# Earlier transposes behind the output projection, and gated MLP weights a chunk ahead, in a two-layer DiT block

## The reference, cut to what matters

```python
x = _layer_norm(DEEPNORM_ALPHA * x + g_a * y, ln1_g[l], ln1_b[l])
x = _layer_norm(DEEPNORM_ALPHA * x + g_m * _squared_relu_mlp(x * (1 + sc_m) + sh_m, mlp_w1[l], mlp_w2[l]),
                ln2_g[l], ln2_b[l])
```

## Time and profile before

| | us |
|---|---|
| median of 3 runs | 3045.91 (3042.36 to 3052.49) |
| profiled execution | 3046.93 |
| its span | 3045.1 |
| around the span | 1.8 |
| PE busy in the span | 2802.1 |
| DVE, ACT, POOL busy | 1397.4, 878.6, 559.6 |
| layer 0 projection begins (first large loads issued) | 524.8 |
| layer 1 projection begins | 2184.3 |
| layer 1, first matmul of the MLP / first second product | 2297.6 / 2337.5 |

### The profile page before, as it was taken

The page is one execution under the profiler, slowest core; times in us unless marked ns, Lnnn a source line. Parts: engine busy times, 40 slices in busy tenths (PEclk is TensorE's granted clock), DMA queues, the critical chain, the costliest instruction groups (busy, mean ns, idle before and its releaser), DMA issues. The chain is left out here.

```text
span 3045.1 us, 40518 instructions
## 1 busy us (share of the span) xinstructions
PE 2802.1 (92%) x15572; PEld 2288.9 (75%) x15572; DVE 1397.4 (46%) x2153; ACT 878.6 (29%) x1684; POOL 559.6 (18%) x375
## 2 busy tenths in 40 slices
PE   5999993999999999999957999999698999999997
PEld 2666783778888888888845888888576888888886
DVE  3575435563333333333383555555555433333345
ACT  4243323342111121121224344343433211121222
POOL 0000002232112121121140000000033323233231
PEclk6999996999999999999977999999999999999999
DMA  6575214541101011010033111110356111111112
GB/s 219 195 301 166 73 52 158 165 132 49 35 28 55 28 41 41 28 55 28 30 122 96 42 36 49 36 36 8 105 131 173 48 46 44 55 41 41 55 41 56
DMA packets 192607, 238.90 MB, mean 78 GB/s; under 512 B 15960, under 2 KB 153776, under 8 KB 186352
## 3 DMA queue, kind: packets, MB, share of 16 engines
q1 hardware_dynamic: 192208, 237.29, 24.4%
q10 hardware_dynamic: 288, 0.10, 0.0%
HBM read 203.70 MB, written 37.88 MB: 79 GB/s over the span
## 5 line engine op out<-in xcount | busy, mean ns | idle before, releaser
L2054 DVE TENSOR_TENSOR y<-y,pair 128x1024 f32<-128x1024 f32 x280 | 340.1, 1219 | 314.1 <-PE pair L2161 314.1
L2159 PE MATMUL pair<-m_wbh,m_ath 128*128 128x512 f32 x1152 | 452.6, 393 | 15.0 <-DVE y L2054 8.4
L2161 PE MATMUL pair<-m_wbh,m_atl 128*128 128x512 f32 x1152 | 451.2, 392 | 0.0
L2160 PE MATMUL pair<-m_wbl,m_ath 128*128 128x512 f32 x1152 | 450.0, 391 | 0.0
L2103 DVE TENSOR_TENSOR m_atl<-m_sq,m_ath 128x512 fp32r<-128x512 f32 x160 | 138.4, 866 | 664.9 <-POOL m_sq L1972 664.0
L1932 ACT ACTIVATE m_rel<-pair 128x512 f32<-128x512 f32 x160 | 88.9, 556 | 996.7 <-PE pair L2183 986.3
L1972 POOL TENSOR_TENSOR m_sq<-m_rel 128x512 f32<-128x512 f32 x160 | 155.7, 973 | 1138.1 <-ACT m_rel L1932 1137.9
L2181 PE MATMUL pair<-hth,m0n_wah 128*128 128x512 f32 (+1 forms) x768 | 273.0, 355 | 2.8 <-ACT m_rel L1932 2.8
L2182 PE MATMUL pair<-htl,m0n_wah 128*128 128x512 f32 (+1 forms) x768 | 273.3, 356 | 0.0
L2183 PE MATMUL pair<-hth,m0n_wal 128*128 128x512 f32 (+1 forms) x768 | 273.2, 356 | 0.0
L2159 PEld LDWEIGHTS pair<-m_wbh,m_ath 128*128 128x128 f32 x1152 | 216.7, 188 | 70.1 <-DVE y L2054 16.8
(11 more groups left out here) (256 smaller groups left out, 5158.5 us busy)
## 6 DMA issues: line engine op xcount, KB each, us to landing
a_ring<-in_w_mod SPq DMA_DIRECT2D x40, 1024.0 KB, 9.1
m_rawb<-in_mlp_w SPq DMA_DIRECT2D x64, 512.0 KB, 4.2
m_rawa<-in_mlp_w SPq DMA_DIRECT2D x60, 512.0 KB, 4.2
x_rows<-r_res SPq DMA_DIRECT2D x28, 512.0 KB, 3.1
r_raw<-cat_cols SPq DMA_DIRECT2D x18, 512.0 KB, 6.0
mod_w<-in_w_mod SPq DMA_DIRECT2D x8, 1024.0 KB, 12.2
r_xin<-in_x SPq DMA_DIRECT2D x16, 512.0 KB, 3.6
gate_pre<-a0g_gout SPq DMA_DIRECT2D x20, 256.0 KB, 2.0
```

What stands on the lines that cost most here:

```text
L2054: dve.tensor_tensor(k.y[:, t, :], k.y[:, t, :], k.pair[t % 2][:, :], ALU.add).then_inc(s_y, 1)
L2159: pe.matmul(o, ath[:, m, ts], wbh[:, m, cols], start=m == 0, stop=False)
L2160: pe.matmul(o, ath[:, m, ts], wbl[:, m, cols], start=False, stop=False)
L2161: i = pe.matmul(o, atl[:, m, ts], wbh[:, m, cols], start=False, stop=m == M - 1)
```

## The change

In `stage_block`, for both layers:

- PE turns the rows as soon as they are normalised (`s_dve`, 6 for each tile), not once POOL has applied weight and shift. POOL applies them afterwards, and now waits for the transposes, since it works in place.
- The weight and shift of the norm go into the modulation's columns instead: two more small loads ahead of the projection weights, one small transpose, one copy and three small DVE operations on 128x8x2 columns; ACT's `modulate` waits for these.
- The last tile's transposes move forward, from ahead of group 1 of the first chunk to behind the first 24 matmuls of group 0.

For layer 1 alone:

- `begin_y` takes only two tiles, not six, between the last two `split_ht`.
- SP loads the first chunk's second weights right behind the gate row, ahead of the residual tiles and of the last store.
- POOL gates a chunk's second weights (L1966) as the chunk begins, not ahead of the last group.

```diff
+    lnr, lnc, lnt = rb("lnr", [2 * KT, P]), rb("lnc", [P, 2, KT]), rb("lnt", [P, KT, 2])
...
             cat_in(0)
+            for i, name in enumerate(("ln1_g", "ln1_b")):
+                sp.dma_start(lnr[i * KT:(i + 1) * KT, :], io[name][layer].rearrange("(k p) -> k p", p=P)).then_inc(s_lnr, 16)
...
                                  bass.AP(tensor=k.gate_dram.tensor, offset=(layer * 2 + 1) * 2 * KT * P, ap=[[0, P], [2 * P, KT], [1, P]])).then_inc(s_grow, 16)
+                    sp.wait_ge(s_dve, C * t + 2)
+                    for m in range(M):
+                        sp.dma_start(rawb[:, m, :], w2[m * P:(m + 1) * P, :]).then_inc(s_rawb[m], 16)
...
                 for m in range(M):
+                    if final and starts(c):
+                        continue
...
                 act.wait_ge(s_tr, t + 1)
+                act.wait_ge(s_fold, 4)
...
                 pool.wait_ge(s_dve, C * t + 6)
+                pool.wait_ge(s_tr, t + 1)
                 pool.tensor_tensor(r, r, lng[:, :], ALU.mult).then_inc(s_g, 1)
...
+                if final:
+                    for m in range(M):
+                        if starts(c):
+                            pool.wait_ge(s_grow, 16)
+                        wait(pool, s_rawb[m], 16 * (c + 1))
+                        pool.tensor_tensor(rawb[:, m, :], rawb[:, m, :], growt, ALU.mult).then_inc(s_bg, 1)
                 for g, (a, n) in enumerate(groups):
-                    if final and g == NG - 1:
-                        for m in range(M):
-                            if starts(c):
-                                pool.wait_ge(s_grow, 16)
-                            wait(pool, s_rawb[m], 16 * (c + 1))
-                            pool.tensor_tensor(rawb[:, m, :], rawb[:, m, :], growt, ALU.mult).then_inc(s_bg, 1)
...
+            dve.wait_ge(s_lnt, 1)
+            dve.tensor_copy(lnc[:, :, :].rearrange("p i j -> p (i j)"), k.bank[7][:, 0:2 * KT]).then_inc(s_fold, 1)
+            dve.wait_ge(s_fold, 1)
+            dve.tensor_tensor(lnt[:, :, :], scale, column(1), ALU.mult).then_inc(s_fold, 1)
+            dve.wait_ge(s_fold, 2)
+            dve.tensor_tensor(shift, shift, lnt[:, :, :], ALU.add).then_inc(s_fold, 1)
+            dve.tensor_tensor(scale, scale, column(0), ALU.mult).then_inc(s_fold, 1)
...
-            begin_y(0 if final else 2, XT - 2 if final else XT)
+            begin_y(0 if final else 2, 2 if final else XT)
             split_ht(tiles - 1)
-            begin_y(XT - 2 if final else XT, tiles)
+            begin_y(2 if final else XT, tiles)
...
             def transposes(t):
-                pe.wait_ge(s_b, t + 1)
+                pe.wait_ge(s_dve, C * t + 6)
...
+            pe.wait_ge(s_lnr, 32)
+            pe.transpose(k.bank[7][:, 0:2 * KT], lnr[:, :], k.ident[0:2 * KT, 0:2 * KT]).then_inc(s_lnt, 1)
...
-                        if g == 1:
-                            transposes(tiles - 1)
                         pe.wait_ge(s_hl, tiles_of(g)[-1] + 1)
...
                         jj = g * M + m
+                        if starts(c) and jj == 1:
+                            transposes(tiles - 1)
```

More of the change, by code:

```diff
@@ L1728, in stage_block @@
     s_dve, s_std, s_g, s_b, s_tr, s_mod, s_hh, s_hl, s_half = [rsem(x) for x in ("dve", "std", "g", "b", "tr", "mod", "hh", "hl", "half")]
+    s_lnr, s_lnt, s_fold = rsem("lnr"), rsem("lnt"), rsem("fold")
     s_store = [rsem(f"store{i}") for i in range(2)]
@@ L2012, in _ @@
                 dve.tensor_tensor(wl[:, u, :], raww[:, u, :], f32(wh[:, u, :]), ALU.subtract).then_inc(s_wlow, 1)
+            scale, shift = [k.mod[:, layer, part * KT:(part + 1) * KT, :] for part in (SC_M, SH_M)]
+            column = lambda i: lnc[:, i, :].unsqueeze(2).broadcast_to([P, KT, 2])
+            dve.wait_ge(s_lnt, 1)
[5 more added lines that the diff above has]
+            dve.tensor_tensor(scale, scale, column(0), ALU.mult).then_inc(s_fold, 1)
             dve.wait_ge(s_row, 64)
```

## The result

| | before | after |
|---|---|---|
| median of the runs, us | 3044.97 (3042.36 to 3052.49) | 3087.69 (3083.86 to 3089.18) |
| ratio, 95% interval | | 1.0135 (1.0122 to 1.0148) |
| span of the profiled execution | 3045.1 | 3082.1 |
| layer 0: first load of the projection to first second product | 173.8 | 195.3 |
| layer 1: the same | 153.6 | 179.5 |

The change costs 42.7 us where +10 was forecast, outside the range. The lower three rows say where: +21.5 and +25.9 us in the two projections with their ends, -8.9 in the last MLP loop. The loop did what was said of it (-9.4). The projections with their ends were to lose 9.2 and 9.9 us (0.8 each for the loads in that) and lost 12 and 16 us more.

What follows compares the result with a forecast made beforehand. PE was taken as the bound, with a second ring as long. 1.6 + 8.4 + 9.1 - 9.4 = +9.7 us on the profiled 3046.93 gives 3056.6, taken as 3056; range 3040 to 3065 (the forecast's own 3051 to 3061).

Steps and rivals of the forecast that it cites:

- The loop: Layer 1's MLP loop: gating as a chunk begins removes a 0.63 us wait of PE 15 times, -9.4 us.
- the loads: Two small loads ahead of each layer's projection weights: +0.8 us twice, +1.6 in all (0 to 2.4).
- Transposes earlier, POOL later: Projection loop: POOL's 4.9 us a tile move by 6 us into the next tile's work; +8.2 layer 0, +6.5 layer 1.
- the meetings at the ports: POOL and DVE at shared ports: the first runs, the other waits for its end, then needs 1.08 (DVE) or 2.24 (POOL).
- The ring's terms: Projection loop, split_ht to split_ht: residual +0.86, split_ht +0.67, ring 11.42 to 12.95 us, against PE's 12.09.
- It stands idle for nothing: Projection loop before the change: PE's round of 12.09 us is 11.01 of matmuls and 1.08 of transposes, without idleness.
- The first collision: Fourth tile's round in the projection loop: one low part falls behind a whole POOL multiply, round 15.7 us, not 11.8.
- rival B: Fourth round: the low part wins the ports, saving 2.2 us a layer; no change, 3050 us, 14 in 100.
- The end of layer 0: Last tile: last norm 11.2 us later, PE stands 4.8 us for it; net +8.4 us (5 to 12).
- The end of layer 1: Last tiles: gate row 10.0 us later, last store lands 12.6 later; +9.1 us (4 to 13) with the lower clock.
- Rival A: Projection loop: nothing collides, residual and split_ht pass POOL freely, rounds about 11.85; faster, 3034 us, 13 in 100.
- Rival C: Worse: late stores, further stops at the lower clock, or the loop's wait stays; +14 to +19, 3062 us, 15 in 100.

Runs made afterwards that it cites:

- e1: The changed kernel with SP issuing each tile's store one round later, behind the next round's loads: 3057.77 us, ratio 1.0044 against the kernel before.
- e4: The changed kernel with stores a round later and POOL's multiply and addition on 8 of 1024 columns only: 3030.78 us, ratio 0.9958 against the kernel before.
- e2: The kernel before with only the gating of a chunk's weights moved to the chunk's beginning, except in the first chunk: 3033.47 us, ratio 0.9963.
- e9: The changed kernel with POOL's addition on 8 of 1024 columns only, its multiply in full: 3060.29 us, ratio 1.0051 against the kernel before.

## Why the prediction was wrong, point by point

*The step that failed* is in "Transposes earlier, POOL later": "POOL's 4.9 us for tile t move ... by 6 us, into the next tile's residual and split_ht." What was counted of this move were the meetings at the ports. Not counted was the queue that POOL's end releases: SP's store of tile t, and behind it in the same list the next input load, with 2.4 to 3.8 us to spare in layer 1 and 5.0 in layer 0, against a move of 7.1. The prediction counts just that for the last tile ("the gate row goes out at 2309.9 instead of 2299.87"), and forgets it for the other tiles. e1 takes this out and lands on the forecast: 3057.77 measured, 3056 forecast. Part of how well it lands is luck: of the 10.7 us by which e1's profiled span exceeds the one before, 3.0 lie ahead of layer 0's projection, where nothing was changed; the two stages and the last loop make 7.7 + 10.7 - 10.4 = +8.0, forecast +9.7.

*The ring's terms were right.* Residual 2.11 (+0.86 forecast, 0.89 measured), split_ht 1.86 (+0.67, 0.69), the round 13.00 (12.95), POOL's multiply 2.9 to 3.4 and addition 3.26, all in e1's settled rounds, where nothing else disturbs them. The ports behave as rows 3 said. e1's layers lose 7.7 and 10.7 us to the second product, forecast 9.2 and 9.9 (8.4 and 9.1 with 0.8 each for the loads). One reading was wrong without harm to the sum: "It stands idle for nothing", said of PE's round of 12.09 us. In the first three rounds of each layer, and all through e4, a round is 11.8 us; in the later ones PE's first matmul comes 1.10 us after the transposes' start instead of 0.79, 0.15 us after the low part's end. The ring set the pace before the change already, so all that was added to it was lost.

*The first collision.* "One low part ... falls behind the whole of a POOL multiply" was right as a mechanism, wrong in how often. In e1 it happens in neither layer: layer 0's rounds, from transposes to transposes, go 11.8, 12.0, 13.4, 13.0 us, where 15.7 was forecast for one; in the third round the low part starts at 593.54 and the multiply at 593.66, and 0.12 us are enough to go first. That is rival B's condition. Its mark are rounds that cost 6.4 us in layer 0 and 4.6 in layer 1 against the kernel before, forecast 7.7 and 6.0. In layer 0 of the changed kernel the late load makes it happen every second round, and the prediction named this as a sign of being wrong ("if one low part more or less falls behind POOL"). Such a pair of rounds takes 30.19 us, 6.0 more than before: 4.75 - 1.08 = 3.7 for the stop and 2.8 for the lower clock, less 0.6 because PE otherwise works at 11.8 us a round. 1.7 was forecast for two rounds.

*The end of layer 0.* In e1 PE waits 4.5 us for the last norm, forecast 4.8. In the changed kernel it waits 2.5, since PE is late itself.

*The end of layer 1.* Here the queue was counted and its direction was right; sizes were off because all came later. The gate row is issued at 2345.52. From there the kernel before takes 37.6 us to the second product (rows 6), this one 37.8 (to 2383.36). PE stands 9.0 us for the weight split. The two weight splits take 4.04 us, not 2.4: they meet POOL's squares (2378.89, 3.33 us), which was not in the sum. In e1 the gate row goes out 126.9 us after the projection's start instead of 116.0, so 10.9 later (forecast 10.0, and 0.8 for the loads), and 37.4 us pass from there to the second product (forecast 36.6). In the changed kernel it goes out 141.6 us after the start: 25.6 later, which is nearly all of layer 1's +25.9.

*The loop* was right: -8.9 in the changed kernel, -9.8 in e2, -9.4 forecast. In the meetings shown here a DVE operation with two SBUF inputs waited for POOL's end, or POOL for its. The rule of the Trainium skill, SBUF: State Buffer, section SBUF: two separate sides, that the shared ports are an exclusive lock, spoke for a slower kernel; the traces agree (2.11 and 1.86 us in e1). Rival A (nothing collides) is out by e1 and e4, 27 us apart. Rival C named the "late stores" and "further stops at the lower clock", but priced them at +19 at most.

*What stays open.* In layer 0 the load is late by 1.78 us once, and from then on by 0.2 or less while the stops go on. That the ring then keeps itself in that phase, by way of the late gate, is read from the rows; no run takes away the first lateness only. Why a load takes 5.8 to 7.7 us in layer 1 and about 5 in layer 0 was not tried either, nor why 7 matmuls are slow behind one stop and 14 behind another.

## What to carry to other kernels

When an operation moves, write down what its end releases, and then the whole rest of the queue in which the released instruction stands: a store that waits in SP's list holds up every load behind it. For each of these note by how much it is early today; a move of 7 us against 2 to 4 us to spare is the finding, and it can be read before anything is built. And in a loop whose ring is as long as the bound, a small lateness may not be paid once: here, as far as the rows show, it shifted the phase of two engines so that they met in every second round.

## What the runs showed that I had not expected

- A load of one input tile lands 5.8 to 7.7 us after its issue in layer 1's loops (before, after, e1, e9), and some 5 in layer 0.
